# Narrow matmuls moved between the products of the first merge, the memory's loads moved from ScalarE's queue to SyncE's, and the convolution steps on VectorE cut into two runs

## What is computed

```python
# first layer: output heads normed, and the two branches merged
o = rmsnorm(o, sub_norm_g) * (1.0 - lam_init)          # per head of 128 columns, 8 heads
merged = g_a * (y_a @ w_up_a) + g_b * (y_b @ w_up_b)   # "the first merge"
x = x + merged @ w_out
...
# second layer
kc = rms_norm(compress_blocks(k_c, ...)); vc = compress_blocks(v_c, ...)
u = a * sigmoid(ag)                                     # convolution: 31 taps, 512 channels
u = conv(u, conv_w) + conv_b
q = rms_norm(heads(q_nsa)); qm = rms_norm(q_mem)
kvm = rms_norm(mem, norm_mem) @ w_mem_kv                # mem: 256 rows of 1024, "the memory"
```

## Time and profile before

| | |
|---|---|
| median of 3 runs | 1837.14 us (1835.72 to 1837.79) |
| the profiled execution | 1837.65 us, its span 1836.0 us |
| mean granted TensorE clock | 0.988 of 2.4 GHz |
| PE (TensorE matmuls) busy | 1801.9 us, 98% |
| PEld (weight loads, beside PE) | 1341.5 us, 73% |
| DVE (VectorE) | 839.8 us, 46% |
| ACT (ScalarE) | 588.5 us, 32% |
| POOL (GpSimd) | 777.1 us, 42% |
| DMA | 266 MB, mean 145 GB/s |

### The profile page before, as it was taken

One profiled execution on the slowest core, in us unless ns is written; L12 is line 12 of the kernel. 1 busy time (PEld: TensorE's weight loads), 2 busy tenths in 40 slices (PEclk: granted clock), 3 DMA queues, 4 the chain that ended last, 5 costly groups with the idle time before them and its releaser, 6 DMA issues.

```text
span 1836.0 us, 23455 instructions
## 1 busy us (share of the span) xinstructions
PE 1801.9 (98%) x8795; PEld 1341.5 (73%) x8795; DVE 839.8 (46%) x1273; ACT 588.5 (32%) x1105; POOL 777.1 (42%) x632
## 2 busy tenths in 40 slices
PE   9999999999999999999999999999999999999999
PEld 6888777775888444443778687777788878888887
DVE  4122665455453243332633769997458352212211
ACT  3223345443233111110232355554462322212220
POOL 4454333333441100000341568887826544544542
PEclk9999999998999999999999999999999999999999
DMA  6222222224243899999533342222254323233221
GB/s 231 94 80 91 91 86 70 87 80 150 92 135 129 296 390 358 361 409 386 210 110 107 101 137 69 70 70 70 87 189 154 111 81 103 92 97 99 92 92 46
DMA packets 81896, 266.37 MB, mean 145 GB/s; under 512 B 8320, under 2 KB 9344, under 8 KB 81792
## 3 DMA queue, kind: packets, MB, share of 16 engines
q1 hardware_dynamic: 64608, 230.31, 35.6%
q10 hardware_dynamic: 14880, 26.22, 4.0%
q0 software_dynamic: 2304, 8.39, 1.3%
HBM read 248.11 MB, written 16.78 MB: 144 GB/s over the span
## 4 chain that ended last, share of the span: by engine, by line
PE 91%; DVE 4%; DMA 2%; POOL 1%; ACT 1%; issue 1%; ACTq 0%; SPq 0%; POOLq 0%; DVEq 0%
PE psum L596 88%; DMA more<-stream 1%; PE psum L967 1%; PE psum L1360 1%; PE psum L728 1%; POOL ring_lo L480 1%; DVE area L2065 1%; DVE area L2606 1%; DVE area L2124 1%; PE psum L925 0%; ACT area L1521 0%; DMA area<-tokens,idx 0%; DVE negm L2105 0%; PE psum L1082 0%; ACT root L1521 0%
## 5 line engine op out<-in xcount | busy, mean ns | idle before, releaser
L596 PE MATMUL psum<-area_r,ring_hi 128*128 128x512 f32 (+1 forms) x3168 | 996.5, 396 | 8.9 <-POOL ring_lo L480 4.2
L480 POOL TENSOR_TENSOR ring_lo<-ring,ring_hi 128x512 fp32r<-128x512 f32 x436 | 592.8, 1383 | 807.7 <-ACT ring_hi L1521 803.0
L596 PEld LDWEIGHTS psum<-area_r,ring_hi 128*128 128x128 f32 x3168 | 589.4, 189 | 146.7 <-issue 23.6
L596 PE MATMUL psum<-area_r,ring_lo 128*128 128x512 f32 (+1 forms) x1584 | 617.4, 390 | 0.0
L1521 ACT ACTIVATE ring_hi<-ring 128x1024 fp32r<-128x1024 f32 x218 | 229.8, 1057 | 570.5 <-PE psum L596 532.2
L596 PEld LDWEIGHTS psum<-area_r,ring_lo 128*128 128x128 f32 x1584 | 299.2, 189 | 63.0
L1521 ACT ACTIVATE area<-psum 128x512 f32<-128x512 f32 (+3 forms) x254 | 124.6, 516 | 262.1 <-PE psum L596 82.6
L2049 DVE RECIPROCAL root<-root 128x512 f32<-128x512 f32 (+1 forms) x30 | 94.1, 3137 | 94.9 <-ACT root L1521 94.9
L596 PE MATMUL psum<-area 128*64 128x128 f32 (+6 forms) x832 | 111.8, 344 | 2.8 <-DVE area L2050 0.8
L596 PE MATMUL psum<-ring,area 128*64 128x512 f32 (+1 forms) x416 | 106.7, 606 | 0.4 <-issue 0.2
L529 POOL DMA_INDIRECT area<-tokens,idx x16 | 15.7, 982 | 204.0 <-DVE idx L2341 161.9
(11 more groups left out here) (222 smaller groups left out, 1636.2 us busy)
## 6 DMA issues: line engine op xcount, KB each, us to landing
ring<-stream SPq DMA_DIRECT2D x324, 512.0 KB, 3.5
more<-stream SPq DMA_DIRECT2D x48, 1024.0 KB, 8.8
gates<-root ACTq DMA_DIRECT2D x24, 256.0 KB, 2.0
area<-gates SPq DMA_DIRECT2D x24, 256.0 KB, 5.8
gates<-area ACTq DMA_DIRECT2D x16, 256.0 KB, 2.3
area<-gates ACTq DMA_DIRECT2D x16, 256.0 KB, 5.6
area<-xT SPq DMA_DIRECT2D x8, 256.0 KB, 4.4
area<-xT ACTq DMA_DIRECT2D x8, 256.0 KB, 3.6
```

The costliest lines, as they stand in the source:

```text
L480: ins = nc.gpsimd.tensor_tensor(ring_lo[:, c % RS, n], ring[:, c % R, n], ring_hi[:, c % RS, n].bitcast(F32), ALU.subtract)
L596: return nc.tensor.matmul(out, lhsT, rhs, start=first, stop=last)
```

## The change

It moves the eight head-square sums into the second chunk of the first merge, one after each group of three products; the first four spreads into the second half of the third chunk; the last four into the fourth chunk, after every second group. It issues the memory's loads on SyncE's queue behind the first six loads after the experts. It cuts VectorE's steps 0 to 29 into 0 to 13 and 14 to 29, with a wait between them for the low halves of chunks `CMP1` and `CMP1 + 1`.

```diff
@@ -397,6 +397,8 @@
             for c in range(MOE1, MOE1 + R):
                 sp.wait_ge(weights_used, c - RM + 1)
                 load(c, c % R)
+            for k in range(KD):
+                sp.dma_start(mem_tiles[:, k, :], memT[k]).then_inc(mem_in, 16)
             segment(MOE1 + R, CMP0 + R, w_lo, R - 1 + MOE1 - MOE0)
             segment(CMP0 + R, CMP1 + R, weights_used, R - 1)
             MERGE = C0["merge2"] + 9
@@ -604,11 +606,13 @@
             def parts(c, lo, hi):
                 return ring_hi[:, c % RS, lo:hi], ring_lo[:, c % RS, lo:hi]
 
-            def by_tile(c, bank, rhs, n=T, off=0, nk=KD, used=True):
+            def by_tile(c, bank, rhs, n=T, off=0, nk=KD, used=True, between=None):
 
                 wait_chunk(c)
                 for k in range(nk):
                     ins = mm3(psum[:, bank, 0:n], parts(c, off + P * k, off + P * k + P), rhs(k), k == 0, k == nk - 1)
+                    if between is not None:
+                        between(k)
                 if used:
                     ins.then_inc(weights_used, 1)
                 return ins
@@ -834,20 +838,29 @@
                     mm(psum[:, 4 + h % 4, :], area[0:8, PT + 2 + h // 4, P * (h % 4):P * (h % 4) + P],
                        root[0:8, 0, :], True, True).then_inc(S("on_bc"), 1)
 
+            def head_squares(h):
+
+                pe.wait_ge(S("onsq"), h + 1)
+                mm(psum[0:8, 6, :], pick[:, 7 - h:15 - h], tile(ONSQ[h]), h == 0, h == 7).then_inc(S("onsum"), 1)
+
+            def spread_early(k):
+
+                if k == 4:
+                    pe.wait_ge(S("on_rec"), 2)
+                if k >= 4:
+                    spread(k - 4, k - 3)
+
+            def spread_late(k):
+
+                if k % 2 == 1:
+                    spread(4 + k // 2, 5 + k // 2)
+
             pe.wait_ge(S("ya_split"), 8)
             for m in range(KD):
-                if m == 1:
-                    for h in range(8):
-                        pe.wait_ge(S("onsq"), h + 1)
-                        mm(psum[0:8, 6, :], pick[:, 7 - h:15 - h], tile(ONSQ[h]), h == 0, h == 7).then_inc(S("onsum"), 1)
-                elif m == 2:
-                    pe.wait_ge(S("on_rec"), 2)
-                    spread(0, 4)
-                elif m == 3:
-                    spread(4, 8)
-                elif m >= 4:
+                if m >= 4:
                     pe.wait_ge(S("bank_read"), 8 + m - 3)
-                by_tile(C0["merge1"] + m, m % 4, rhs_of((YAH, YAL)))
+                by_tile(C0["merge1"] + m, m % 4, rhs_of((YAH, YAL)),
+                        between={1: head_squares, 2: spread_early, 3: spread_late}.get(m))
             pe.wait_ge(S("onout"), 8)
             for m in range(KD):
                 if m >= 4:
@@ -1830,8 +1843,6 @@
             act.wait_ge(weights_used, C0["vsw"] + 2)
             for j in range(2):
                 A(tile(VSW + j), psum[:, 2 + j, :], ACT.Copy).then_inc(S("vsw_out"), 1)
-            for k in range(KD):
-                act.dma_start(mem_tiles[:, k, :], memT[k]).then_inc(mem_in, 16)
             normed("kv", kv_entries())
             for j in range(2):
                 follow(C0["kv2"] + 3 + j)
@@ -2514,7 +2525,9 @@
                 V.tensor_tensor(upad[:, c, TAPS - 1:TAPS - 1 + T], tile(SCR2 + c % 2), psum[:, 4 + 2 * (c % 2), :],
                                 ALU.mult).then_inc(S("conv_u"), 1)
             dve.wait_ge(S("conv_u"), CONVT)
-            conv_taps(0, 30)
+            conv_taps(0, 14)
+            dve.wait_ge(w_lo, split_no(CMP1 + 1) + 1)
+            conv_taps(14, 30)
             dve.wait_ge(S("cmp_root"), 1)
             link(V.reciprocal(root[0:64, 0, 0:2 * NCMP], root[0:64, 0, 0:2 * NCMP]))
             for g in range(2):
```

## The result

| | before | after |
|---|---|---|
| median | 1837.68 us (8 runs, 1835.72 to 1839.14) | 1842.95 us (8 runs, 1836.12 to 1851.77) |
| ratio | | 1.0036, 95% interval 1.0023 to 1.0048 |
| the profiled execution | 1837.65 us, span 1836.0 | 1843.17 us, span 1841.6 |
| mean granted clock | 0.988 | 0.985 |

The account below looks back on a forecast made before the run. TensorE (PE), busy 1801.9 of 1836.0 us, was taken as the bound. Merge +3.4, loads -1.1 and taps -5.6 sum to -3.3, so 1837.14 becomes 1833.8 us; range 1829.5 to 1840.5.

Parts of the forecast that it names:

- The merge: First merge, sums and spreads moved between products: +3.4 us, bounds -4.0 and +14.6.
- a change of shape: First merge, each excursion to narrow matmuls and back: 0.30 us for a sum, 0.40 for a spread, +4.5 extra.
- the wait: First merge, PE waits ahead of the first spread for VectorE's reciprocal, its cover being shortened: +0.6 us.
- a fall in the third chunk: First merge, the clock falls to 0.50 in the third chunk for about 6.8 us: +3.4 us.
- rivals 3: First merge: clock falls in the third chunk, comes back mid-fourth; +7 in place of +3.4, 1837.4 us, chance 0.19.
- Rival 4: First merge: clock stays low from the first spreads to the fourth chunk's end; +14.6, 1845 us, slower, chance 0.14.
- The chain of eight heads: First merge, VectorE's chain, some 2 us a head, ends before the sixth chunk needs its second bank: costs nothing.
- The loads: First kv sum: with the memory's loads off ScalarE, PE's 1.04 us idle goes; -1.1 us.
- The taps: Start of q2, tap steps in two runs: -4.1 idle, -2.6 clock, +1.1 new wait, -5.6 us; bounds -6.7 and -1.
- The row of 10.756 us disagrees: q2's taps: GpSimd's first low half, held 10.756 us, did not get in between any two of some 14 steps.
- rival 5: q2: second run of taps collides with GpSimd's low halves; -2 instead of -5.6, 1837 us, chance 0.07.
- "Slower": Whole kernel slower than before, decided by a merge loss from 10.4 us (3.7 + 6.7) on; chance 0.14.

Follow-up runs that it names:

- e1: The kernel before with only the merge part of the change; median 1844.39 us, ratio 1.0044 to before.
- e13: The whole change with 10 of the tap steps moved behind q2's first square sum; median 1839.52 us, ratio 1.0010 to before.
- e2: The kernel before with the loads on SyncE and the taps in two runs, the merge unchanged; median 1837.37 us, ratio 0.9998 to before.
- e8: The change, but sums and spreads as whole 128x128 matrices in the places of the kernel before; median 1833.03 us, ratio 0.9967 to before.
- e10: e2 with ten of the tap steps moved behind q2's first square sum; median 1830.12 us, ratio 0.9949 to before.
- e3: The whole change with the spreads padded by zeros from 8 to 128 rows; median 1838.09 us, ratio 1.0002 to before.
- e9: The whole change with sums and spreads as whole 128x128 matrices, between the products as in the change; median 1836.47 us, ratio 0.9982 to before.
- e5: The kernel before with only the memory's loads moved to SyncE's queue; median 1835.56 us, ratio 0.9988 to before.
- e4: The kernel before with only the taps cut into two runs; median 1839.84 us, ratio 1.0011 to before.

## Why the prediction was wrong

**The merge (+3.4 forecast; +9.9 in the profile, +8.1 by e1's ratio).** The terms held: 0.31 and 0.42 a change of shape (0.30 and 0.40 taken), 0.59 for the wait (0.6). What failed is the last step, the length of the fall: "a fall in the third chunk that lasts about as long as the first one now, 6.8 us". It lasted 20.5 us in after and 23.9 in e1 and e13. The text had the reason against itself in the sentence before, spreads among the products of the fourth chunk too (1.36 of products to 1.26), and gave it to rivals 3 and 4. With the half of 20.5 in the place of 3.4, its sum is 4.5 + 0.6 - 5.1 + 10.25 = 10.25 against 9.9 measured. Rival 4 is what happened in the profiles, for some 10 us and not 14.6, since the clock fell 5.2 us after the first spread's start and not with it, and came back with the last spread and not behind it. The price taken was that of a fall with products behind it: in before spreads run at 0.50 for 2.4 us only (441.0 to 443.4 in the earlier trace rows), then products alone; in after spreads and products by turns fill the 20.5.

In the merge the clock of after, e1 and e13 falls with PE busy: in after its last idle, 0.52 us, ends at 445.28, 5.2 us ahead of the fall. At q2 it fell in e2 and e8, where PE stood 5.5 and 5.3 us, and stayed in e10, where it did not stand. So the Trainium skill's rule that idle gaps throttle (TensorE: Matmul & The Clock Gate, HAM oscillation) agrees with the traces at q2, and does not account for the falls in the merge.

**The chain of eight heads, put at "nothing".** Wrong, but hidden: with the clock kept, e3 and e9 show 0.9 us of wait for it at the sixth chunk. In after the slow clock covered it.

**The loads (-1.1).** -1.3 in the traces of all kernels that have them, -2.2 (0.6 to 3.9) by e5's ratio. Right, and so was the gap on SyncE's queue, though the eight issues took 6.29 us there and not some 3.7.

**The taps (-5.6).** -5.2 in after's profile, the wait 1.2 for 1.1: each step as drawn. Yet it is one outcome of two. By e4's ratio the part costs 2.0 (0 to 4.0), by its trace 0.2. What failed is the sentence "The row of 10.756 us disagrees": one row of one meeting of the two engines was read as how they always meet, and rival 5 (C about -2, 0.07) got the little that was left. Its own working, four pieces of 1.25 us that push the taps, PE up to 5 us more, is what six profiles show. Even it, -1 to -2, was too good by 1 to 3 us in the traces (+0.2 to +0.9): it left out that the clock falls behind that wait, for 3.4 us in e2 and 6.8 in e8.

**The range and the chances.** "Slower" hung on rival 4 alone, from a loss of 10.4 us in the merge on. That bound took the taps' -5.6 for given: with +2.0 in their place it is 2.8 us, and even the forecast's own +3.4 lies beyond. Two uncertain terms were weighed one at a time, with the other at its best guess.

## What to carry to other kernels

Where narrow matmuls stand among full ones and the clock has once fallen behind them, price a move that spreads them out at the whole stretch over which they then lie, not at the length of the fall seen; and try the same matmuls padded to 128 rows first: here that took away both the cost of changing shape and the fall. A gain that needs two engines to meet in one of two ways has to be timed over many executions, since one profile shows only one of them; better is to move the work so that they do not meet. Before matmuls are moved to fill gaps, look at what their old neighbours were covering.

## What the runs showed that was not expected

- Padding made the rounds cheaper: a round of one spread and three products takes 1.96 us with 8 rows and 1.55 with 128, a round of one sum 1.85 with 8 columns and 1.55 with 128.
- The granted clock fell in a stretch where PE was busy throughout with 8-row spreads and products by turns (after, e1, e13), and did not with 128-row spreads in the same places (e3, e9); 8-column sums with 128 rows did not lower it either (1.00 from 426 to 450.5 in after).
- Back-to-back two-input steps of VectorE and GpSimd's subtraction meet in two ways: GpSimd held for 7.8 to 10.8 us at no cost to VectorE, or both by turns, most pieces at 1.7 and most steps at 1.8 us for what takes 1.27 and 0.75 alone. Seven profiles with the steps in two runs: one and six. Four with one long run: all held.
- The times from lowest to highest lie 15.7 us apart in after, 14.4 in e1 and 10.3 in e13, with 8-row spreads among the products, and 6.6 in e3. But e4 and e8, without them, lie 12.2 and 11.7 apart, so the spreads are not shown to be the reason.
